# Expert activations of a hybrid decoder layer: dot products spread evenly over the tiles, run with less lag, splits in quarters, and the last gate stores in one place

## The reference, cut to what matters

```python
def block(xb):                                  # 128 tokens
    ...                                         # scores, top 16 of each half, top 16 of the sums
    e = jnp.take_along_axis(cand_idx, g_i, axis=-1)     # (tokens, 8 heads, 16) expert numbers
    g = jax.nn.softmax(g_s, axis=-1)
    act = jax.nn.gelu(jnp.einsum('thed,td->the', u[e], xb))
    return jnp.einsum('the,thed->td', g * act, v[e])
```

## Time and profile before

| what | value |
|---|---|
| runs | 2392.18, 2396.69, 2404.06 us |
| median | 2396.69 us |
| the profiled execution's own time | 2392.18 us |
| its span | 2390.5 us |
| mean granted TensorE clock | 0.923 |
| busy over the span | PE 88%, DVE 68%, POOL 41%, ACT 36% |
| `stage_activate` with its columns | about 1089 to 1832 us |

### The profile page before, as it was taken

The page is one execution under the profiler, slowest core; times in us unless marked ns, Lnnn a source line. Parts: engine busy times, 40 slices in busy tenths (PEclk is TensorE's granted clock), DMA queues, the critical chain, the costliest instruction groups (busy, mean ns, idle before and its releaser), DMA issues. The chain is left out here.

```text
span 2390.5 us, 32219 instructions
## 1 busy us (share of the span) xinstructions
PE 2093.0 (88%) x10417; PEld 1680.4 (70%) x10417; DVE 1634.7 (68%) x2980; ACT 853.0 (36%) x1717; POOL 982.6 (41%) x855
## 2 busy tenths in 40 slices
PE   8998995677896676999999879988896999999997
PEld 7774682343445454889899879977885788888885
DVE  3562105868331223589699989988876899988888
ACT  1232011033201111113576656646672333333331
POOL 1000242312100000006688779877896555544440
PEclk9998997678898777999999989999998999999999
DMA  5323437946613211234588878878999999999993
GB/s 194 77 58 113 118 109 267 334 160 231 250 52 106 79 45 44 62 104 154 180 289 289 266 243 300 283 255 266 324 320 341 375 396 405 398 382 390 386 387 136
DMA packets 243760, 547.73 MB, mean 229 GB/s; under 512 B 22174, under 2 KB 126287, under 8 KB 242346
## 3 DMA queue, kind: packets, MB, share of 16 engines
q1 hardware_dynamic: 114538, 287.33, 34.9%
q0 software_dynamic: 60736, 208.40, 23.9%
q10 hardware_dynamic: 68352, 50.34, 6.4%
HBM read 485.51 MB, written 60.02 MB: 228 GB/s over the span
## 5 line engine op out<-in xcount | busy, mean ns | idle before, releaser
L2079 POOL DMA_INDIRECT u_gather<-in_u_rows,gather_ids x160 | 205.5, 1284 | 533.8 <-DVE gather_ids L1889 419.0
L2087 POOL TENSOR_TENSOR uL<-u_raw,uH 128x512 fp32r<-128x512 f32 x256 | 387.2, 1535 | 64.5 <-ACT uH L2005 36.2
L2426 PE MATMUL psum<-hH,uH 128*128 128x384 f32 x1024 | 357.4, 349 | 42.9 <-POOL uL L2087 42.8
L2426 PE MATMUL psum<-hH,uL 128*128 128x384 f32 x1024 | 349.2, 341 | 0.0
L2426 PE MATMUL psum<-hL,uH 128*128 128x384 f32 x1024 | 348.8, 341 | 0.0
L2534 POOL DMA_INDIRECT v_gather<-in_v_rows,idx_now x160 | 235.3, 1471 | 252.1 <-DVE y_sample L2619 157.5
L2666 PE MATMUL psum<-vH,wH 128*128 128x512 f32 x768 | 300.9, 392 | 21.9 <-DVE wL L2612 21.9
L2321 DVE CUSTOM_DVE_ANT_0 u_gather<-u_gather,h 128x1024 f32<-128x1024 f32 x160 | 268.3, 1677 | 58.7 <-DMA u_gather<-in_u_rows,gather_ids 48.8
L2666 PE MATMUL psum<-vL,wH 128*128 128x512 f32 x768 | 300.0, 391 | 0.0
L2666 PE MATMUL psum<-vH,wL 128*128 128x512 f32 x768 | 300.0, 391 | 0.0
L2426 PEld LDWEIGHTS psum<-hH,uH 128*128 128x128 f32 x1024 | 197.6, 193 | 49.3 <-POOL uL L2087 48.9
(11 more groups left out here) (484 smaller groups left out, 3455.0 us busy)
## 6 DMA issues: line engine op xcount, KB each, us to landing
u_raw<-in_uT SPq DMA_DIRECT2D x128, 512.0 KB
S<-in_v_rows SPq DMA_DIRECT2D x64, 512.0 KB
v_rest<-in_v_rows SPq DMA_DIRECT2D x64, 512.0 KB
activation_table<-acts ACTq DMA_DIRECT2D x128, 192.0 KB
gate_table<-Gtile ACTq DMA_DIRECT2D x48, 512.0 KB
S<-gate_table SPq DMA_DIRECT2D x16, 768.0 KB
S<-activation_table SPq DMA_DIRECT2D x16, 768.0 KB
G_rest<-gate_table SPq DMA_DIRECT2D x16, 768.0 KB
```

Of the source, the lines that this page charges most:

```text
L2079: c.nc.gpsimd.indirect_dma_start(c.ug[:, k % RG], None, c.A["u_rows"].rearrange("j i d -> (j i) d"), bass.IndirectOffsetOnAxis(ap=c.ids[:, ...
L2087: ins = c.nc.gpsimd.tensor_tensor(c.uL[:, n % RU, d], c.u[:, n % RAW, d], c.uH[:, n % RU, d].bitcast(F32), ALU.subtract)
L2426: ins = nc.tensor.matmul(column[n % 4][:, 0:ND], w[:, n % RU, d], x[:, d], start=m == 0, stop=m == len(parts) - 1)
```

## The change

Four things are altered: how many dot slots each step has, how many slots later DVE runs a dot (6, then 4), the split of a column's low part (two pieces of 512 elements per partition, then four of 256), and the place of the last four gate stores (one at each of four tail columns, then all four at the first). All counts of columns, gathers, dots and bytes stay: 160 dots before and after.

```diff
-STEP_DOTS = ((1, 1, 1) + (0,) * 5, (6,) * 7 + (5,), (7, 6, 6, 6) * 2, (7, 6) * 4)
+STEP_DOTS = ((1,) * 8, (6, 5) * 4, (6,) * 8, (7, 6) * 4)
...
-DOT_LAG = 6
+DOT_LAG = 4
...
 def low_u(c, n):
-    for d in (slice(0, KD // 2), slice(KD // 2, KD)):
-        ins = c.nc.gpsimd.tensor_tensor(c.uL[:, n % RU, d], c.u[:, n % RAW, d],
-                                        c.uH[:, n % RU, d].bitcast(F32), ALU.subtract)
+    for d in range(0, KD, 2):
+        ins = c.nc.gpsimd.tensor_tensor(c.uL[:, n % RU, d:d + 2], c.u[:, n % RAW, d:d + 2],
+                                        c.uH[:, n % RU, d:d + 2].bitcast(F32), ALU.subtract)
     ins.then_inc(c.u_split, 1)
...
-                flush(i)
                 if i == 0:
+                    flush()
                     gates_out(STILE)
...
-                def flush(i):
-                    if i == 0:
-                        evict(NUNIT - 1)
-                    if i < STORES:
+                def flush():
+                    evict(NUNIT - 1)
+                    for i in range(STORES):
                         store(NTB - 1, i)
```

## The result

The change makes the kernel slower: 2437.97 us in the median (2434.70 to 2441.92) against 2399.05 (2392.18 to 2404.06), a ratio of 1.0165, interval 1.0133 to 1.0198. That is +39 us where -13 was forecast, and above the range. The profiled execution took 2436.38 us with a span of 2434.7, 44.2 longer than the span before.

The account below looks back on a forecast made before the run. The prediction took PE and DVE as nearly full in tiles 1 and 2, with a DVE, POOL, PE chain behind the largest holes. Terms -16 - 4 + 0 + 7 + 0 = -13 us gave a 2384 us median, range 2360 to 2414.

Parts of the forecast that it names:

- Lag at the tile ends, -16: Ends of tiles 1 and 2: POOL splits two more columns ahead, PE's holes shrink, DVE gains 7 + 9 us.
- a rival of its own (0.12): Tile ends give nothing: DVE alone sets tile 2's first unit at 1405.05; +3 us, 2400, chance 0.12.
- Lag in tile 3, +7: Tile 3: dots need gathers two slots sooner, so DVE waits on the chain; 0 to +16 us, taken as 7.
- Three turns in two steps: Tile 3: chain from compare through ACT, POOL and gather to dot, 16.1 us each, 49.5 per two steps against 45.4.
- the stated worst case: Tile 3: four pairs of steps each lengthened by the chain from compare to dot, +16 us at the most.
- The cover that was named for tiles 1 and 2: Tiles 1 and 2: three units, 16.2 us, just cover the compare-to-dot chain; priced 0, up to 16 us if lost.
- Quarters, 0: POOL's low part in four pieces: extra POOL time and DVE's relief set at 6 us each; ends -15 and +20.
- the POOL rival: Tiles 1 to 3: four pieces give POOL 100 us more work and make it the bound; +20, 2417, chance 0.17.
- Dots into tile 0, -4: Four dots move into DVE's waits in tile 0, leaving five fewer where DVE is full in tile 1; -4 us.
- Stores at once, 0: First tail column: three more store issues on ACT, covered by POOL's gathers; 0 us, from -2 to +3.
- The joint case of POOL and the turns (0.08): POOL becomes the bound and tile 3's compare-to-dot chain also costs time; up to 2425, chance 0.08.
- what was to show the steps right: PE's holes about 3 us, tile 2 and 3 first units 7 and 9 earlier, tile 0 dots, mean compare under 1.3.

## Why the prediction was wrong, by its own steps

**Lag at the tile ends, -16: wrong, and the first cause of the sign.** The prediction filled PE's hole and took 7 + 9 us of it over into the time. The hole did shrink (11.41 to 4.59 us with the lag alone), the time to the next tile's first unit by 1.6 and 0.8. The step that failed is "PE then reaches the transposes earlier, and DVE can use it": behind the last pick DVE runs 25.5 us of its own work without a wait, so nothing that PE does earlier counts. That was the lower bound of the term and a rival of its own (0.12). The 4.92 us of the earlier trace rows that spoke against it did go, and DVE's operations beside POOL's work took as much longer (4.8). In the change itself the stretch is 1.6 us shorter after tile 1 and 5.1 after tile 2; at the first of them DVE did wait 6.41 us for PE, so that with quarters PE's hole counts after all.

**Lag in tile 3, +7: the mechanism right, the size wrong, and the second cause.** Three turns in two steps were priced at 49.5 us; with the lag alone six steps took 148.0 us, 49.3 for two. Two steps before were taken as 45.4 from one pair; the mean of three pairs is 131.4 / 3 = 43.8. So the loss was that of the stated worst case, +16.5 us in tile 3, though the equality is chance: it is three pairs of steps at 5.5, not four at 4.1. Taking 7 leaned on a shorter turn; 14.8 and 15.5 us could be read, but over the six steps no less than forecast. The cover that was named for tiles 1 and 2, three units of 5.4 against a turn of 16.1, is no cover at a margin of 0.1 us: priced at 0 with 16 if it goes, the two tiles lost 6.2 + 12.0 = 18.2, of which DVE's waits for gathers account for 3 in tile 1 and for all in tile 2. That the two ends named, 16 + 16 = 32, equal the 32 us measured is in part luck.

**Quarters, 0: the terms that were mis-sized are POOL's contended time and where DVE's relief goes.** Uncontended the piece came out as worked out: 0.72 forecast, 0.712 the shortest, 0.742 the median. By the Trainium skill (GPSIMD Engine Reference, 3.1) a two-input operation takes about 2.6 cycles per element at a clock of 1.2 GHz, from which an estimate for 256 elements is 0.55 us. The trace agrees: the shortest pieces of 512 and 256 differ by 1.251 - 0.712 = 0.54. But a column grew by 0.89 us and not 0.38, over 108 columns 96.5 us, nearly the 100 of the POOL rival. DVE's relief was 37 us, also more than allowed, and counted for nothing: POOL issues the gathers between its columns, and DVE's waits for them rose by 78. The rival was right in its price and half right in its place: POOL did not reach 95% (202 of 225 us in tile 1, 90%), and PE's waits for the low part rose by only 10 us from 1185 to 1640 us with quarters alone (14 when each kernel's tiles 1 and 2 are taken to their end), DVE's waits for gathers by 46. The Trainium skill (SBUF — State Buffer, "SBUF: two separate sides") calls the shared pair an exclusive lock, held for the whole instruction. The trace agrees: what a compare loses grows with the piece, 1.476 - 0.955 = 0.52 us with pieces of 256 (medians) and 1.08 with pieces of 512. The rival had drawn the consequence that the term of 0 left out: with smaller pieces POOL meets a busy DVE more often, and a column waits 1.12 us where it waited 0.58.

**Dots into tile 0, -4: half right.** Tiles 1 and 2 gave 4.9 and 2.0 us. The gathers' wait for dot k - 3 at a lag of 6, which the prediction wrote down for the tile ends, was not applied to tile 0, and cost 12.9 us there. At lag 4 tile 0 is still 6.0 us longer (the change) and 3.5 (the change with halves), but not by that wait: POOL's gathers wait 6.1 us for a dot in both, where they waited 5.0 before. What costs it was not separated.

**Stores at once, 0:** within its bounds.

**The sum.** With the sizes of the single runs it would have read 32 (lag, ends and turns together) + 29 + 7 + 2 = +70 and still have missed: in tiles 1 and 2 most of the losses do not add, and the change costs 39. The joint case of POOL and the turns (0.08) came nearest, at up to 2425; it left the turns of tiles 1 and 2 out. Range and chances did not fit each other either: the POOL rival at 2417 (0.17) and the joint case (0.08) both lie above the range's end of 2414. Of what was to show the steps right, the mean compare (1.28), the dots in tile 0 and one of PE's two holes came (2.45 us after tile 2); the other did not (4.59 with the lag alone, 9.48 in the change), and the time did not follow. Of what was to show them wrong, DVE's wait for gathers came (139.8 for 48.8).

That the ring sets tile 3 is shown by the distances: with six, seven, eight and nine slots from gather to dot it takes 152.6, 140.3, 136.1 and 127.9 us, the lag being 4 in the first two. How much of the loss in tiles 1 and 2 under quarters is PE's wait for a low part and how much is DVE's for a gather was not separated; no run has quarters with nine slots.

## What to carry to other kernels

Before a lag or a ring is shortened, count the slots from a transfer's issue to its use and follow the whole ring of engines round once: a cover of 16.2 against 16.1 us was none here, and a term whose worst case has a mechanism should be priced there. Where single parts do not add up to the whole, compare them stretch by stretch: here they add in tile 3 and hardly in tiles 1 and 2. A hole on one engine is worth only what the engine behind it can use: look whether that engine has a wait at the place. Splitting GpSimd's work helped VectorE and cost GpSimd more than its fixed part. Two pieces instead of one paid where VectorE had no room (tiles 1 and 2), four instead of two paid nowhere, and one piece paid where VectorE had room (tile 3).

## What the runs showed of the hardware

A column's low part on POOL took 2.62 us in one piece, 3.08 in two and 3.97 in four in the mean, where the shortest pieces add up to 2.35, 2.50 and 2.85. The waiting is the rest, 0.27, 0.58 and 1.12 us a column: of what a split adds, some six tenths are waiting. One column of four pieces took 5.57. The compare beside it took 1.86, 1.42 and 1.31 us in the mean.

The longest compare hardly depends on the split. It is 3.373 us with halves, and with quarters alone and with one piece:

```profile
L2349 DVE TENSOR_TENSOR hT<-iota,bcol x96: 945/1472/3649, 1185.6 to 1813.5; 128x768 f32<-128x768 f32 x96
L2347 DVE TENSOR_TENSOR hT<-iota,bcol x96: 945/953/3575, 1185.2 to 1809.3; 128x768 f32<-128x768 f32 x96
```

In all three it started while POOL was still issuing a gather, at most 0.4 us before the first piece, and ended 0.8 us after the last: behind two pieces (compare from 1406.80, pieces from 1406.85 to 1409.34 in the kernel before), behind four (from 1653.73, pieces 1653.78 to 1656.55) and behind one (from 1421.81, piece 1422.21 to 1424.56). So the engine that is blocked does not always come in between two pieces.

A gather of 512 KB issued at 1708.25 in the kernel after and one at 1724.40 ended DVE's wait 5.7 and 5.1 us later.
